# Per-expert gates of an inference step: scattered by adding DMAs into a zeroed DRAM table in place of one-hot products on TensorE

## The chip, the cores and the metric

One core of a Trainium2 chip runs the whole step in one launch. Times are device microseconds, from three runs for the kernel before; a profiled execution is a further run with the hardware profiler on. Lower is better. The engines are PE (TensorE: matmuls, with PEld its weight loads), DVE (VectorE), ACT (ScalarE), POOL (GpSimd) and SP (which only issues DMAs). All DMAs run on the same 16 DMA engines: those that SP issues stand in the profile as hardware_dynamic (q1), those that POOL issues as software_dynamic (q0).

## The reference

The model is one layer: two mixers (RWKV-7 and Mamba-2) and then a product-key expert layer, for 576 tokens (512 of a prompt and 64 of a sample) of width 1024. The change touches only the expert layer:

```python
q = (xn @ w_q).reshape(bsz, t, P_HEADS, 2, P_QDIM // 2)            # 8 heads, 2 sides
s = jnp.einsum('bthcd,ckd->bthck', q, sub_keys).astype(jnp.float32)  # 128 keys a side
sv, si = lax.top_k(s, P_TOPK)                                        # 16 of each side
cand = (sv[..., 0, :, None] + sv[..., 1, None, :]).reshape(bsz, t, P_HEADS, P_TOPK * P_TOPK)
cand_id = (si[..., 0, :, None] * N_KEYS + si[..., 1, None, :]).reshape(bsz, t, P_HEADS, P_TOPK * P_TOPK)
top_s, top_pos = lax.top_k(cand, P_TOPK)                             # 16 of 256 pairs
eid = jnp.take_along_axis(cand_id, top_pos, axis=-1)                 # of 16384 experts
gate = jax.nn.softmax(top_s, axis=-1).astype(xn.dtype)
# for each token and each of its 8 * 16 picks e:
hid = jnp.einsum('td,ted->te', xb, u_tab[eb])
out = jnp.einsum('te,ted->td', jax.nn.gelu(hid, approximate=False) * gb, v_tab[eb])
```

So each token picks 128 of 16384 experts, with a gate for each. An expert that two heads pick for a token gets the sum of both gates.

## The kernel before, in words

**Dense and sparse tokens.** The first 128 tokens (SP) are treated sparsely in the second layer: their 128 picks are gathered row by row. The other 448 tokens (DN) are treated densely: TensorE multiplies them with all 16384 experts, and gates that are zero for all but the picks weigh the hidden values in between. The 16384 experts are 128 "keys" of 128 experts. Each product of 32-bit values is three matmuls on halves (high by high, low by high, high by low: lines 126 to 128, `three_products`); the halves are made by ACT (high) and by POOL or DVE (low).

**The stages, in order of time.** (1) Input projection and the mixers, tile of 128 tokens by tile. Meanwhile SP copies the v table from its argument to scratch in DRAM (`VRows`, 512 KB for each key; `MIX_COPIES` says how many of the 128 copies are issued in which tile: 74 in the mixers, 54 later). (2) Output projection. (3) Routing, `route`: 54 jobs on PE, 16 of them query projections and 38 (`AHEAD4`) hidden keys of the first expert layer that are computed ahead. For each of the eight heads DVE takes the top 16 of each side, then of the 256 sums; POOL's `match_keys` (line 1953) turns ranks into key numbers, two for each head. POOL also makes the low half of every job's weights (`split_low`, line 260), and DVE in `finish_picks` the gates. ACT makes the high half of job j+1 when job j-1 has left PE, and POOL's low half must be there when PE comes to job j+1. (4) Spreading the gates, `spread_gates`: the picks are transposed by PE (`turn_picks`), then for each of the 448 dense tokens DVE compares its 128 picks' first and second keys with a row of key numbers, which gives two 128 by 128 one-hot matrices, one of them scaled by the gates (the scaling is ACT's and DVE's), and PE multiplies them (line 2279): the product is the token's 128 by 128 table of gates. ACT moves it out of PSUM, SP stores it. In between PE computes 14 (`AHEAD5`) further hidden keys. (5) The hidden stage, `act_hidden` and its like: the remaining 76 (`NC_KEYS`) hidden keys; DVE multiplies each key's hidden values with its gates (`make`), and SP stores the product (`prod`). (6) The output stage, `pe_out` and its like: for each key SP loads v (512 KB) and the product w (224 KB), ACT and DVE split both, PE multiplies (24 matmuls). Meanwhile POOL gathers, for the sparse tokens, one value (`value_of_pick`) and one row of v (`row_ring`, 512 KB for 128 tokens) for each of their 128 picks, and DVE adds the weighed row up (line 2711). (7) The last normalization and the stores.

**What sets the order.** Every engine runs its program in order and waits on semaphores; there is no planner. On POOL the order is: splits and matches of the routing jobs, then the splits of hidden keys, then 16 values, then rows and values in turn. A row's gather waits until its slot of 16 (`RING`) is free and until the row three before it has landed (`IN_FLIGHT`). SP's order is written out in `sp_route`, `sp_spread`, `sp_hidden`, `sp_out`.

## Time and profile before

| | |
|---|---|
| median of 3 runs | 2288.07 us (2275.89 to 2293.09) |
| the profiled execution's own time | 2283.04 us |
| its span (first to last instruction) | 2281.2 us |
| granted TensorE clock, mean | 0.977 |
| PE busy | 2184.2 us, 96% |
| DVE busy | 1293.3 us, 57% |
| ACT busy | 882.9 us, 39% |
| POOL busy | 924.2 us, 41% |
| DMA | 478.86 MB, mean 210 GB/s |
| expert layer's stages, from the trace | routing jobs 542 to 922, gates 922 to 1112, hidden 1112 to 1599, output 1599 to 2265 |

A busy share is a mean over stages with different limits: DVE is over 90% busy from 1000 to 1100 us and 15% from 1200 to 1300 us. Matmuls overlap each other in PE, so a matmul's own duration (295 ns) is more than what it adds to the time; how many start in a stretch tells its rate.

### The profile page before, as it was taken

The page shows a single profiled execution, that of the slowest core. Times are in us where ns is not written, and L with a number is a line of the kernel's source. Part 1 is how long each engine was busy: PE and PEld are TensorE (multiplying, and loading weights), DVE is VectorE, ACT ScalarE, POOL GpSimd, SP SyncE. Part 2 cuts the span into 40 slices and gives each one's busy share as a digit, 9 for nine tenths or more (in the row PEclk, how much of TensorE's full clock was granted, in tenths as well). Part 3 has the DMA queues.
Part 4 walks back from the last instruction along what each step waited for, and adds up shares of the span by engine and source line. Part 5 has one row for each costly group of instructions (what it writes and reads, how often), then busy time and mean ns, then how long its engine had stood idle before and what let it go on. Part 6 is the DMA issues. An engine that isn't in the chain of part 4 may idle for free.

```text
span 2281.2 us, 41950 instructions
## 1 busy us (share of the span) xinstructions
PE 2184.2 (96%) x16703; PEld 2069.1 (91%) x16703; DVE 1293.3 (57%) x2471; ACT 882.9 (39%) x1722; POOL 924.2 (41%) x555
## 2 busy tenths in 40 slices
PE   8997888998999999999999999999979999999997
PEld 7996777888999999999999999999759999999996
DVE  4563666656798996899421111112336666666666
ACT  5235445535333333899522222222213333333332
POOL 1433344432445455211233333333765656564300
PEclk9999999898999999999999999999979999999999
DMA  3548366525666566476867677766678888888842
GB/s 129 179 135 242 92 203 190 160 84 171 183 189 193 187 189 187 154 227 218 288 238 256 234 243 239 259 227 224 227 241 275 270 276 275 271 276 269 268 150 82
DMA packets 298806, 478.86 MB, mean 210 GB/s; under 512 B 31168, under 2 KB 227584, under 8 KB 298504
## 3 DMA queue, kind: packets, MB, share of 16 engines
q1 hardware_dynamic: 276104, 409.25, 54.6%
q0 software_dynamic: 22528, 67.19, 9.5%
q8 instruction: 122, 2.00, 0.4%
q14 instruction: 52, 0.43, 0.1%
HBM read 383.86 MB, written 159.60 MB: 238 GB/s over the span
## 4 chain that ended last, share of the span: by engine, by line
PE 73%; DVE 2%; issue 1%; DMA 1%; ACT 1%; POOL 0%; SPq 0%; DVEq 0%; ACTq 0%; POOLq 0%
PE banks L126 22%; PE banks L128 22%; PE banks L127 22%; PE banks L2279 4%; PE banks L1968 1%; DMA u_raw<-arg_u 1%; DVE n_y L342 0%; DMA scratch_gates<-gate_stage 0%; DVE res_x L2763 0%; DVE res_lo L349 0%; DVE n_sq L383 0%; DVE n_inv L335 0%; DVE gates_in L2760 0%; ACT res_hi L1823 0%; POOL u_low L1784 0%
## 5 line engine op out<-in xcount | busy, mean ns | idle before, releaser
L126 PE MATMUL banks<-res_hi,u_high 128*128 128x288 f32 x1456 | 438.2, 301 | 2.8 <-POOL u_low L2156 1.7
L128 PE MATMUL banks<-res_hi,u_low 128*128 128x288 f32 x1456 | 428.9, 295 | 0.0
L127 PE MATMUL banks<-res_lo,u_high 128*128 128x288 f32 x1456 | 428.8, 295 | 0.0
L127 PE MATMUL banks<-w_low,v_high 128*128 128x448 f32 x1024 | 379.3, 370 | 7.7 <-issue 7.7
L126 PE MATMUL banks<-w_high,v_high 128*128 128x448 f32 x1024 | 379.4, 370 | 6.6 <-issue 6.3
L128 PE MATMUL banks<-w_high,v_low 128*128 128x448 f32 x1024 | 379.9, 371 | 5.5 <-issue 5.4
L2156 POOL TENSOR_TENSOR u_low<-u_raw,u_high 128x1024 fp32r<-128x1024 f32 x75 | 181.2, 2416 | 303.8 <-ACT u_high L2152 303.8
L2678 DVE TENSOR_TENSOR gated<-gelu_out,gates_in 128x448 f32<-128x448 f32 x76 | 48.2, 634 | 408.3 <-ACT gelu_out L2635 390.6
L126 PEld LDWEIGHTS banks<-res_hi,u_high 128*128 128x128 f32 x1456 | 273.5, 188 | 3.2 <-POOL u_low L2156 2.0
L127 PEld LDWEIGHTS banks<-res_lo,u_high 128*128 128x128 f32 x1456 | 273.6, 188 | 0.1
L128 PEld LDWEIGHTS banks<-res_hi,u_low 128*128 128x128 f32 x1456 | 273.0, 188 | 0.0
L2788 POOL DMA_INDIRECT row_ring<-scratch_v_rows,expert_of_pick x128 | 188.3, 1471 | 187.4 <-DVE row_total L2711 166.9
L126 PE MATMUL banks<-res_hi,q_wh 128*128 128x288 f32 x864 | 257.7, 298 | 1.4 <-DVE res_lo L349 1.2
L128 PE MATMUL banks<-res_hi,q_wl 128*128 128x288 f32 x864 | 255.3, 295 | 0.0
L127 PE MATMUL banks<-res_lo,q_wh 128*128 128x288 f32 x864 | 255.1, 295 | 0.0
L2626 ACT ACTIVATE w_high<-w_raw 128x448 fp32r<-128x448 f32 x128 | 74.0, 578 | 458.7 <-PE banks L128 400.0
L2671 DVE TENSOR_TENSOR w_low<-w_raw,w_high 128x448 fp32r<-128x448 f32 x128 | 79.9, 625 | 266.3 <-ACT w_high L2626 243.1
L128 PEld LDWEIGHTS banks<-w_high,v_low 128*128 128x128 f32 x1024 | 193.8, 189 | 30.2 <-issue 11.3
L127 PEld LDWEIGHTS banks<-w_low,v_high 128*128 128x128 f32 x1024 | 193.9, 189 | 28.6 <-issue 9.6
L126 PEld LDWEIGHTS banks<-w_high,v_high 128*128 128x128 f32 x1024 | 193.8, 189 | 27.5 <-issue 8.6
L260 POOL TENSOR_TENSOR q_wl<-q_raw,q_wh 128x1024 fp32r<-128x1024 f32 x54 | 130.0, 2409 | 179.3 <-ACT q_wh L256 179.3
L2635 ACT ACTIVATE gelu_out<-banks 128x288 f32<-128x288 f32 x152 | 54.1, 408 | 354.5 <-PE banks L128 354.5
(424 smaller groups left out, 4594.7 us busy)
## 6 DMA issues: line engine op xcount, KB each, us to landing
scratch_v_rows<-arg_v SPq DMA_DIRECT2D x128, 512.0 KB, 8.2
v_raw<-scratch_v_rows SPq DMA_DIRECT2D x128, 512.0 KB
u_raw<-arg_u SPq DMA_DIRECT2D x37, 1024.0 KB, 5.5
scratch_gates<-gate_stage SPq DMA_DIRECT2D x14, 2048.0 KB, 7.5
scratch_prod<-gated SPq DMA_DIRECT2D x128, 224.0 KB, 3.2
w_raw<-scratch_prod SPq DMA_DIRECT2D x128, 224.0 KB
q_raw<-arg_u SPq DMA_DIRECT2D x38, 512.0 KB, 4.0
gates_in<-scratch_gates SPq DMA_DIRECT2D x19, 896.0 KB, 5.0
```

The costliest lines, as they stand in the source:

```text
L126: pe.matmul(out, ah, bh, start=first, stop=False)
L127: pe.matmul(out, ah, bl, start=False, stop=False)
L128: return pe.matmul(out, al, bh, start=False, stop=last)
L260: eng.tensor_tensor(self.wl[:, c % self.ring, :], self.raw[:, c % 3, :], self.wh[:, c % self.ring, :].bitcast(F32), ALU.subtract).then_inc ...
L1968: ins = pe.matmul(bank[0:T, (n % 4) * P:(n % 4 + 1) * P], qT[:, c % 2, tok:tok + T], keys[:, c % 2, :], start=True, stop=True)
L2156: pool.tensor_tensor(self.lo[:, jj % 2], self.raw[:, jj // 2, jj % 2], self.hi[:, jj % 2].bitcast(F32), ALU.subtract).then_inc(self.low, 1)
L2279: ins = pe.matmul(core.psum[:, g % BANKS, t * P:(t + 1) * P], pair[:, g % SLOTS, t, :], pair[:, g % SLOTS, FOUR + t, :], start=True, stop= ...
L2626: act.activation(wh[:, k % W_SLOTS, :], w_raw[:, k % W_SLOTS, :], ACT.Copy).then_inc(w_high, 1)
L2635: ins = act.activation(gelu[:, n % G_SLOTS, half * HALF:(half + 1) * HALF], core.psum[:, 2 * (n % 2) + half, 0:HALF], ACT.Gelu)
L2671: dve.tensor_tensor(wl[:, k % W_SLOTS, :], w_raw[:, k % W_SLOTS, :], wh[:, k % W_SLOTS, :].bitcast(F32), ALU.subtract).then_inc(w_low, 1)
L2678: dve.tensor_tensor(blocks(made[:, m % M_SLOTS, :]), blocks(src), gate, ALU.mult).then_inc(made_done, 1)
L2788: pool.indirect_dma_start(out=ring[:, s % RING, :], out_offset=None, in_=core.v_rows.dst.rearrange("k p d -> (k p) d"), in_offset=bass.Ind ...
```

## The change

The gates' table is made in DRAM by DMAs, without TensorE.

- **Table.** `GateRows`: 128 keys by 128 experts by 448 tokens, 29.4 MB. In the mixers SP writes zeros over it, in 32 DMAs of four keys (eight in each of four tiles) from a row of zeros in SBUF. For that only 40 of the v table's copies remain in the mixers; the 34 others follow the routing's, one with each key of the hidden stage.
- **Places.** For each head, DVE in `finish_picks` computes for every pick its place in the table: (second-side and first-side key numbers as an expert number) times 448, plus the token's number. Three small operations more for each head.
- **Scatter.** `Sparse.scatter`: POOL issues an indirect DMA with `compute_op=ALU.add` for one pick of 128 tokens: 128 elements of 4 bytes. There are 16 for each head for each of three full tiles of tokens. The last tile has 64 tokens: half of its picks are moved to the other 64 partitions (`move`, by SP), so that 8 DMAs do for a head. That makes 448. For one tile, a head's DMAs wait until those of the head before have landed, as two heads may pick one expert.
- **Removed.** `spread_gates` altogether: one-hot matrices, their products, the transposes, the stores of the gates, and also the store of the weighed hidden values with their class `Products`. `AHEAD5` is 0: 90 hidden keys (`NC_KEYS`) follow the routing's last job at once.
- **Hidden stage.** The low half of u is made by DVE in place of POOL from the third key on. SP stores the plain hidden values (`hid_dense`). At key 86, SP waits for all scatters (`scattered`) before the first loads of the output stage.
- **Output stage.** For each key SP loads v, the hidden values and the gates (512, 224 and 224 KB), and DVE multiplies the latter two (`weigh_key`) before they are split. A row's gather no longer waits for the row three before it; it waits until PE is within 8 keys (`AHEAD_ROWS`) of the key at which the row is summed up. `W_SLOTS` is 4 in place of 3.

```diff
-AHEAD5 = 2 * G_STEPS
+AHEAD5 = 0
 AHEAD4 = 38
-MIX_COPIES = (0, 18, 38, 58, N_KEYS - (2 * P_HEADS + AHEAD4))
+KEY4 = N_KEYS - AHEAD4
+MIX_COPIES = (0, 10, 20, 30, 40)
+ZEROED = 4
...
+    def scatter(self, pool, h, n, k):
+        last = n == NT - 1
+        if k == 0:
+            pool.wait_ge(self.placed, h + 1)
+            if last:
+                pool.wait_ge(self.moved, 32 * (h // (P_HEADS // 2) + 1))
+            if h:
+                pool.wait_ge(self.done[n - 1], 16 * h * (TOPK // 2 if last else TOPK))
+        c = h * TOPK + k
+        pool.indirect_dma_start(
+            out=self.core.gate_rows.dst.rearrange("k p t -> (k p t)").unsqueeze(1),
+            out_offset=bass.IndirectOffsetOnAxis(ap=self.place[:, n, c:c + 1], axis=0),
+            in_=self.gates[:, n, c:c + 1], in_offset=None, compute_op=ALU.add).then_inc(self.done[n - 1], 16)
...
+                def copy_and_zero(n):
+                    core.v_rows.copy(sp, MIX_COPIES[n], MIX_COPIES[n + 1])
+                    for z in range(8 * n, 8 * n + 8):
+                        core.gate_rows.zero(sp, zeros, z)
...
+        placed_by = {h: job_of_q[2 * h + 4] + 5 for h in range(P_HEADS - 2)}
+        for j in range(len(jobs)):
+            for _ in range(2):
+                if j < len(jobs) - 1 and placed_by.get(sparse.order[core_n][0], len(jobs)) < j:
+                    core_n += 1
+            scattered_by.append(core_n)
...
                 gemm.split_low(pool, j)
                 if j in match_after:
                     match_keys(*match_after[j])
-            spread.first_low(pool)
+                for h, n, k in sparse.order[scattered_by[j - 1]:scattered_by[j]]:
+                    sparse.scatter(pool, h, n, k)
+            for n in range(2):
+                u.split_low(pool, 0, n)
+            for h, n, k in sparse.order[scattered_by[LAST]:]:
+                sparse.scatter(pool, h, n, k)
...
+                e, f = cleft[:, :, 0:TOPK], cleft[:, :, TOPK:2 * TOPK]
+                link(dve.scalar_tensor_tensor(out=e, in0=picks[:, :, 1, hs], scalar=float(N_KEYS), in1=picks[:, :, 0, hs],
+                                              op0=ALU.mult, op1=ALU.add))
+                link(dve.scalar_tensor_tensor(out=f, in0=e, scalar=float(DN), in1=column[:, :, :].broadcast_to([P, NT, TOPK]),
+                                              op0=ALU.mult, op1=ALU.add))
+                dve.tensor_copy(sparse.place[:, :, hs], f).then_inc(sparse.placed, 1)
...
-def spread_gates(core, acts, u, sel, iota, gelu, gelu_sent_ahead, sel_out, gemm):
...
+                if n == NC_KEYS - 4:
                     core.v_rows.ready(sp)
+                    sparse.scattered(sp)
...
+            sp.dma_start(hid[:, k % W_SLOTS, :], core.hid_dense[k]).then_inc(h_in[k % W_SLOTS], 16)
+            sp.dma_start(gate[:, k % W_SLOTS, :], core.gate_rows.dst[k]).then_inc(g_in[k % W_SLOTS], 16)
...
             def row(s):
                 if s >= RING:
                     pool.wait_ge(summed_rows, s - RING + 1)
-                if s >= IN_FLIGHT:
-                    landed(s - IN_FLIGHT)
+                if ROW_KEY[s] > AHEAD_ROWS:
+                    pool.wait_ge(out_done, ROW_KEY[s] - AHEAD_ROWS)
...
             def _(pool):
                 pool.sem_clear(mixing_sems)
                 project.pool(pool)
-                route.pool(pool, spread)
-                spread.pool(pool)
-                for n in range(2, NC_KEYS):
-                    u.split_low(pool, n // JJ, n % JJ)
+                route.pool(pool)
                 pool_rows(pool)
```

POOL's order in the routing, where two heads' matches meet the jobs' splits (`q_wl` is the low half of a job's weights). Before:

```order
L1953 TENSOR_TENSOR rank_match<-rank_match,top_index_f 128x1280
L260 TENSOR_TENSOR q_wl<-q_raw,q_wh 128x1024
L1953 TENSOR_TENSOR rank_match<-rank_match,top_index_f 128x1280
L260 TENSOR_TENSOR q_wl<-q_raw,q_wh 128x1024 x5
L1953 TENSOR_TENSOR rank_match<-rank_match,top_index_f 128x1280
```

And now:

```order
L2020 TENSOR_TENSOR rank_match<-rank_match,top_index_f 128x1280
L265 DMA scratch_gate_rows<-gate_of_pick,place_of_pick 7340032x1 x2
L307 TENSOR_TENSOR q_wl<-q_raw,q_wh 128x1024
L2020 TENSOR_TENSOR rank_match<-rank_match,top_index_f 128x1280
L265 DMA scratch_gate_rows<-gate_of_pick,place_of_pick 7340032x1 x2
L307 TENSOR_TENSOR q_wl<-q_raw,q_wh 128x1024
```

Two scatters follow every job's split and match, from job 14 to job 52: 78 in all.

POOL's order behind the routing, from the last split of the routing to the first gathers. Before:

```order
L2156 TENSOR_TENSOR u_low<-u_raw,u_high 128x1024 x75
L2775 DMA value_of_pick<-scratch_hid,hidden_of_pick 128x1 x16
L2788 DMA row_ring<-scratch_v_rows,expert_of_pick 128x1024
L2775 DMA value_of_pick<-scratch_hid,hidden_of_pick 128x1
```

And now:

```order
L2221 TENSOR_TENSOR u_low<-u_raw,u_high 128x1024 x2
L265 DMA scratch_gate_rows<-gate_of_pick,place_of_pick 7340032x1 x370
L2568 DMA value_of_pick<-scratch_hid,hidden_of_pick 128x1 x16
L2578 DMA row_ring<-scratch_v_rows,expert_of_pick 128x1024
L2568 DMA value_of_pick<-scratch_hid,hidden_of_pick 128x1
```

The splits of the hidden keys have left POOL, and 370 scatters in one piece stand in their place.

## Rows read from the trace of the kernel before

**Rows 1.** The page: the chain that ended last, by line, share of the span

```profile
PE banks L126 22%; PE banks L128 22%; PE banks L127 22%; PE banks L2279 4%; PE banks L1968 1%; DMA u_raw<-arg_u 1%; DVE n_y L342 0%; DMA scratch_gates<-gate_stage 0%; DVE res_x L2763 0%; DVE res_lo L349 0%; DVE n_sq L383 0%; DVE n_inv L335 0%; DVE gates_in L2760 0%; ACT res_hi L1823 0%; POOL u_low L1784 0%
```

**Rows 2.** Windows: length, busy us (x instructions) by engine, PEclk, DMA share, GB/s

```profile
925.00:1110.00 185.00, 185.00 (x1538) 185.00 (x1537) 172.90 (x252) 173.44 (x478) 33.39 (x14) 1.00 0.68 218
1100.00:1200.00 100.00, 97.22 (x743) 96.83 (x742) 22.79 (x30) 33.75 (x69) 33.85 (x14) 1.00 0.79 274
1142.00:1590.00 448.00, 448.00 (x3383) 448.00 (x3383) 73.56 (x122) 117.60 (x212) 170.09 (x71) 1.00 0.70 243
```

**Rows 3.** Windows of the output stage

```profile
1600.00:1700.00 100.00, 80.43 (x333) 65.95 (x332) 35.45 (x38) 22.31 (x29) 68.28 (x61) 0.85 0.73 239
1700.00:1800.00 100.00, 100.00 (x486) 90.81 (x485) 63.26 (x64) 31.02 (x41) 60.52 (x47) 1.00 0.84 274
2165.00:2240.00 75.00, 75.00 (x365) 68.11 (x364) 43.78 (x45) 22.93 (x30) 0.00 (x0) 1.00 0.44 151
```

**Rows 4.** POOL's gathers of one value: count, busy us, mean ns, idle before

```profile
L2775 POOL DMA_INDIRECT value_of_pick<-scratch_hid,hidden_of_pick x128 | 138.8, 1084 | 50.8 <-issue 50.2 <-DMA row_ring<-scratch_v_rows,expert_of_pick 0.6
```

**Rows 5.** Timeline of POOL's gathers: start, us, engine, line [idle before]

```profile
1620.45 1.94 POOL L2775 DMA_INDIRECT value_of_pick<-scratch_hid,hidden_of_pick  x1 [0.30 <-issue]
...
1677.04 0.94 POOL L2775 DMA_INDIRECT value_of_pick<-scratch_hid,hidden_of_pick  x1 [0.30 <-issue]
1684.78 1.68 POOL L2788 DMA_INDIRECT row_ring<-scratch_v_rows,expert_of_pick  x1 [6.80 <-DVE row_total L2711]
```

**Rows 6.** Timeline of POOL in the routing, one head and the next

```profile
721.56 2.40 POOL L260 TENSOR_TENSOR q_wl<-q_raw,q_wh 128x1024 fp32r<-128x1024 f32 x1 [3.96 <-ACT q_wh L256]
726.08 4.14 POOL L1953 TENSOR_TENSOR rank_match<-rank_match,top_index_f 128x1280 f32<-128x1280 f32 x1 [2.13 <-DVE rank_match L2117]
730.19 2.40 POOL L260 TENSOR_TENSOR q_wl<-q_raw,q_wh 128x1024 fp32r<-128x1024 f32 x1
732.55 2.95 POOL L1953 TENSOR_TENSOR rank_match<-rank_match,top_index_f 128x1280 f32<-128x1280 f32 x1
735.74 2.40 POOL L260 TENSOR_TENSOR q_wl<-q_raw,q_wh 128x1024 fp32r<-128x1024 f32 x1 [0.24 <-ACT q_wh L256]
...
767.15 4.16 POOL L1953 TENSOR_TENSOR rank_match<-rank_match,top_index_f 128x1280 f32<-128x1280 f32 x1 [2.13 <-DVE rank_match L2117]
```

**Rows 7.** Timeline of ACT: it takes the job before PE's current one

```profile
734.00 0.41 ACT L2040 ACTIVATE gelu_ahead<-banks 128x288 f32<-128x288 f32 x1 [4.86 <-PE banks L128]
```

**Rows 8.** Window of that head in the routing

```profile
726.00:767.00 41.00, 41.00 (x310) 40.42 (x309) 37.25 (x136) 14.31 (x25) 21.43 (x8) 1.00 0.60 189
```

**Rows 9.** Landing of transfers at `scratch_hid` (stores, value gathers); DVE's groups by form

```profile
DMA to landing us min/median/max: 1.5/2.5/13.4
...
L2080 DVE TENSOR_TENSOR picks<-pick_values,gate_sum 128x80 f32<-128x80 f32 x8 | 1.9, 242 | 0.3
L2666 DVE TENSOR_TENSOR v_low<-v_raw,v_high 128x1024 fp32r<-128x1024 f32 x91 | 110.8, 1217 | 0.0
L2671 DVE TENSOR_TENSOR w_low<-w_raw,w_high 128x448 fp32r<-128x448 f32 x92 | 57.5, 625 | 164.5 <-ACT w_high L2626 164.1 <-issue 0.4
```

**Rows 10.** DMA queues: packets, MB, share; of 1900 to 2000 us

```profile
q1 hardware_dynamic: 5773, 15.12, 44.7%
q0 software_dynamic: 4026, 12.02, 39.1%
```

**Rows 11.** DMA queues of 1640 to 1660 us, and that window

```profile
q0 software_dynamic: 1351, 3.97, 67.2%
q1 hardware_dynamic: 576, 1.51, 19.1%
...
1640.00:1660.00 20.00, 13.16 (x45) 8.31 (x43) 6.09 (x7) 3.05 (x4) 15.73 (x15) 0.90 0.87 274
```

**Rows 12.** Windows where SP's transfers alone fill the DMA engines

```profile
340.00:360.00 20.00, 19.14 (x298) 15.23 (x297) 12.09 (x24) 13.56 (x28) 11.14 (x10) 1.00 1.08 313
1120.00:1140.00 20.00, 19.31 (x148) 19.08 (x146) 2.39 (x4) 5.93 (x12) 6.15 (x3) 1.00 0.94 347
```

570 lines of the change are left out of this document (168 added, 402 removed).

## The prediction

> **What bounds the kernel now.** I read the chain of waits first: three quarters of the span hang on PE, in the three-product matmuls, and 4% on line 2279, the one-hot products [rows 1]. So the question for each part is what it adds to PE's work or to PE's waits. The windows by stage answer that. In the hidden stage PE never pauses: 3383 matmuls in 448 us, 132.4 ns each, and a hidden key of 48 matmuls takes 6.36 us. In the gates' stage PE is as full (185 of 185 us), but its 1538 matmuls take 120 ns each, because more than half of them are one-hot products [rows 2]. The output stage has three faces [rows 3]: from 1700 us on it runs full at 486 matmuls in 100 us (205.8 ns each, 4.94 us a key of 24), also late where no rows are gathered (365 in 75 us, at a DMA share of 0.44 in place of 0.84). But its first 100 us hold only 333 matmuls, at a granted clock of 0.85. That is where POOL issues gathers without a pause, one in 1.25 us (0.94 and 0.30 idle) [rows 5].
>
> **The sum, against the profiled execution's span of 2281.2 us.**
>
> *One-hot products, removed.* A group is four tokens: 8 one-hot matmul records and 6 of the hidden keys (14 keys of 48 over 112 groups). 185 us for 1538 records make 1.684 us for a group of 14 [rows 2]; its hidden part costs 6 x 0.1324 = 0.794. So 0.890 us x 112 = **-99.7 us**. DVE's and ACT's one-hot work (both over 170 of 185 us busy) goes too, but it lay beside PE. The 14 hidden keys move behind the routing at the same price.
>
> *The hand-over to the hidden stage, removed.* Gates' stores and loads fill the DMA engines, and PE is 97.22 us busy of 1100 to 1200 [rows 2]: **-2.8 us**.
>
> *The burst of row gathers, removed.* 333 in place of 486 matmuls: 153 x 0.2058 = 31.5 us. In 1640 to 1660 POOL's queue holds 67% of the DMA engines' time and SP's only 19% [rows 11], where the steady stage gives SP 44.7% [rows 10]. The new wait lets row 0 go at the second finished key and then one in 0.875 key, so no burst of 16 rows can form: **-31.5 us**.
>
> *Scatters in the routing (78).* The trace has no scatter. The nearest instruction is the value gather, also 128 elements of 4 bytes: 0.94 us and 0.30 idle alone [rows 5], 1.084 and 0.30 on average beside DVE [rows 4], 1.94 at worst of those shown, and 1.68 for a row's gather beside DVE [rows 5]. So c, a scatter's whole price, is 1.25 us at the low end and 1.98 (1.68 and 0.30) at the high end. I take 1.3 to 1.4, nearest to the value gathers' mean. POOL is in order: a scatter delays the next job's low half. One head is six jobs, 41.1 us (match to match, 726.08 to 767.15), in which POOL works 21.4 us [rows 6, 8]; 12 scatters at c = 1.25 make that 36.4, at 1.98 45.2. Even where the total fits, the two matches of a head lie on adjacent jobs. With c = 1.25: match to 730.2, two scatters to 732.7, low half to 735.1, but PE wants it at 734.0 (ACT takes the job before it there [rows 7]); match to 738.1, scatters to 740.6, low half to 743.0, wanted at 734.0 + 1.1 + 6.4 = 741.5. PE loses 2.6 us a head, in the six heads with both matches after job 14: 16 us. With c = 1.98 it is 5.5 us a head, 33 us. Nothing at all is the bound below, if POOL catches up. I take **+18**.
>
> *Scatters behind the routing (370).* They cover 370c. At the end come the last tile's four heads, each waiting until the one before has landed: four times about 2.5 us [rows 9] = 10. They must be done before PE ends its 90 hidden keys (90 x 6.36 = 572 us), less some 8 us for the first loads and splits: 564. The break-even is c = (564 - 10)/370 = 1.50 us. At 1.25 they end 91 us early, at 1.38 43 us, at 1.98 they are 179 us late. With c as taken: **0**. The cover is the hidden stage, which DVE leaves idle but for the u splits (73.6 us busy of 448, with work that mostly goes [rows 2]).
>
> *DVE's added work.* Three operations a head like the 242 ns one [rows 9]: 0.7 us in 41 where DVE is 37.25 us busy [rows 8]. The u split, 1.22 us (as v_low) in a key of 6.36. In the output stage one more product of 0.63 us [rows 9] in 4.94, on 63% busy: 76%. **0** for all. SP issues one load more for a key, ACT nothing: 0.
>
> *Zeros and v copies.* A tile of the mixers had up to 20 copies (10.5 MB) and has 10 copies and 8 DMAs of zeros (12.6 MB). At the 313 GB/s that such a burst reaches that is 7 us more of a full queue, while PE ran 19.14 of 20 us beside it [rows 12]. Nothing below, 4 x 7 = 28 above: **+3**. The 34 copies now in the hidden stage bring it to about 211 GB/s (0.82 MB for u and the stores, 0.52 for the copy, in 6.36 us); before it moved 243 [rows 2]: 0.
>
> *Loads of the output stage.* A key needs 512 + 224 + 224 KB: 199 GB/s, and a row in 0.875 key 121: 320 together, where 274 ran before [rows 3]. In time of the DMA engines: SP's 44.7%, of which 224 of 736 KB (13.6%, a little more as its packets are small) come on top: with POOL's 39.1% [rows 10] 97 to 100%. While rows were gathered no 20 us went above 0.87 [rows 11]; with SP alone the share reached 0.94 and 347 GB/s, and 1.08 [rows 12]. So it is on the edge. If 0.87 is the ceiling, a key takes 4.94 x 0.99/0.87 = 5.62 us for some 112 keys: +76. If 1.0 can be had, 0. The windows of SP's queue alone are the nearer ones, since here too SP's loads are the larger part and the row gathers are evenly paced: **+20**.
>
> The Trainium skill, "DMA: Bandwidth & Descriptors", section "Where 436 GB/s comes from", puts HBM's limit for one core at about 358 GB/s; 320 would pass under it, and by that the term is 0 and the sum 20 us lower. The trace agrees so far that SP's queue alone came to 347 GB/s [rows 12].
>
> Sum: 2281.2 - 99.7 - 2.8 - 31.5 + 18 + 3 + 20 = **2188 us** of span. The profiled execution took 1.8 us more than its span, and the median of the runs lies 5.0 us above that execution: **2195 us**.
>
> **Rivals.**
>
> *A: as above,* 2160 to 2225: 0.48.
>
> *B: the scatters become the bound, slower.* Adding makes each element a read, a sum and a write; nothing in the trace prices that, neither on POOL nor in the DMA engines. Place: SP's wait at key 86, behind which hidden stores, gelu and then PE stand. It bites from c = 1.50; each 0.1 us more costs 37 us there. At 1.98: 2195 - 18 + 33 + 179 = 2389 us. Slower than before by over 1% (2311) needs +116, c of about 1.80. For it: it is a guess between two gathers, and only 20% above what I take is harmless. Against: where POOL ran without a pause the gathers held 0.94 us. 0.28, of which 0.19 above 1.80, 0.06 within 1%, 0.03 still faster.
>
> *C: the output stage is bound by DMA:* 2195 - 20 + 76 = 2251 us. For it, SP was starved at a total share of 0.87 [rows 11]; against, POOL's part there was 67%, now 39%. 0.12.
>
> *D: in the routing every scatter stands behind a DVE operation.* DVE is 37 of 41 us busy there [rows 8]; at the 1.94 us seen once, and 0.30, POOL needs 21.4 + 12 x 2.24 = 48.3 in 41.1 us: 7.2 x 6 = 43 us in place of 18, 2220 us. 0.05.
>
> The Trainium skill, "SBUF — State Buffer", section "SBUF: two separate sides", says that DVE operations on two SBUF ports lock GpSimd out of writing descriptors, with about 3100 ns in place of 620 for a DMA so overlapped; by its figure POOL would need 58.6 us a head and the kernel come to about 2282. The trace shows the lock's direction (0.94 against 1.68) but nothing so long.
>
> *E: routing and loads cost nothing:* 2195 - 18 - 20 = 2157 us. 0.07.
>
> **Range and chances.** 2150 to 2320: the bottom takes in E, the top A, C, D and B up to c of about 1.83; it leaves out most of B's 0.19. About 1% (23 us) is what this kernel's runs tell from no change. Faster: A, C, D, E and 0.03 of B, 0.75. Within 1%: 0.06. Slower: 0.19.
>
> **What the changed profile would show.** Line 2279 gone, hidden keys at 132 ns a matmul up to about 1500 us. Scatters near 0.94 to 1.1 us, the last of 370 by about 1450 us, a gap before the value gathers: if they run into the end of the hidden stage instead, with PE idle behind it, B is right. PE waiting on the low half of q twice a head in the routing: the +18. The first 100 us of the output stage as full as the rest: the -31.5. PE or ACT waiting on v or on the product in the middle of that stage, and a DMA share near 1: C. I am wrong at the root if DMA engines take long over an added element, which POOL's issue times would not show but the landing would.

## The result: slower by 5.4%, and the profile after

The changed kernel takes **2413.86 us** (median of 4 runs, 2391.81 to 2416.62) where the kernel before takes 2287.74: a ratio of **1.054** (95% interval 1.046 to 1.061). I had forecast 2195. Rival B named what came, with a chance of 0.19 for a time more than 1% slower.

The page's group of the scatters (columns as in [rows 4]), and its chain by line, to be held against [rows 1]:

```profile
POOL scratch_gate_rows L265 28%; PE banks L121 11%; PE banks L122 11%; PE banks L123 11%; POOL q_wl L307 1%; POOL rank_match L2020 1%; DMA scratch_gate_rows<-gate_of_pick,place_of_pick 1%; DVE candidates_left L2139 0%; DVE n_y L389 0%; PE banks L2040 0%; DVE pick_pos L2120 0%; DVE candidates_left L2109 0%; DVE pick_pos L2110 0%; DVE pick_values L2106 0%; DVE pick_values L2117 0%
...
L265 POOL DMA_INDIRECT scratch_gate_rows<-gate_of_pick,place_of_pick x448 | 764.0, 1705 | 138.8 <-issue 129.4
```

The three-product matmuls held 66% of the chain before and hold 33% now; POOL's scatters, 1.7 us each and 0.30 idle, hold 28%. What waits for them, in PE's list of waits (us in total, times, longest):

```profile
PE banks L121 <- DVE u_low L2221: 216.8, 2, 211.6
PE banks L121 <- POOL q_wl L307: 20.4, 12, 2.3
```

The 211.6 us are one gap, from 1514.5 to 1726.1. `u_low` is named because DVE's last splits stand in its program behind the product of hidden values and gates, and this waits for the first loads of the output stage, which SP issues only when all scatters have landed. The last scatter starts at 1712.57, and DVE's order behind it is:

```profile
1718.94 0.63 DVE L2476 TENSOR_TENSOR gated<-hidden_in,gates_in 128x448 f32<-128x448 f32 x1 [214.23 <-DMA gates_in<-scratch_gate_rows]
...
1724.76 1.22 DVE L2221 TENSOR_TENSOR u_low<-u_raw,u_high 128x1024 fp32r<-128x1024 f32 x1
```

Three windows, in the columns of [rows 2]: the hidden stage, the gap, and the output stage.

```profile
1200.00:1300.00 100.00, 100.00 (x757) 100.00 (x756) 18.41 (x16) 26.54 (x48) 85.63 (x48) 1.00 0.54 130
1520.00:1712.00 192.00, 0.00 (x0) 0.00 (x0) 0.00 (x0) 0.00 (x0) 153.91 (x100) 0.50 0.21 0
1900.00:2000.00 100.00, 100.00 (x485) 90.82 (x484) 73.38 (x84) 30.69 (x41) 53.96 (x48) 1.00 0.92 322
```

Beside the scatters PE runs full, 132 ns a matmul, as in [rows 2]. Then it does nothing while POOL issues its last hundred. The DMA engines don't hold these up: their share is 0.21. The limit is the time POOL needs to issue one. In the output stage PE runs as full as in [rows 3], at a DMA share of 0.92.

By stages, in us, from the first and last matmuls of each in both traces:

| stretch | before | after | difference | forecast |
|---|---|---|---|---|
| start to first routing job | 542.7 | 544.3 | +1.6 | +3 |
| routing jobs (first to last query matmul) | 379.0 | 409.1 | +30.1 | +18 |
| to the output stage, without the gap | 677.4 | 583.7 | -93.7 | -102.5 |
| gap | | 211.6 | +211.6 | 0 |
| output stage | 666.0 | 645.0 | -21.0 | -11.5 |
| end | 16.1 | 16.2 | +0.1 | 0 |
| span | 2281.2 | 2409.9 | +128.7 | -93 |

The gap is the term that was missed, and the routing cost more than forecast. The -21.0 of the output stage hides two errors that partly cancel (see below). The +1.6 ahead of the routing is within what this stage varies from run to run: the first routing job starts at 537 to 554 us in the traces of this document, with zeros and without. In the routing, the timeline of POOL (start, us) shows the price directly:

```profile
704.58 2.95 POOL L307 TENSOR_TENSOR q_wl<-q_raw,q_wh 128x1024 fp32r<-128x1024 f32 x1
707.70 1.55 POOL L265 DMA_INDIRECT scratch_gate_rows<-gate_of_pick,place_of_pick  x1 [0.17 <-issue]
709.56 1.55 POOL L265 DMA_INDIRECT scratch_gate_rows<-gate_of_pick,place_of_pick  x1 [0.31 <-issue]
710.56 2.97 POOL L307 TENSOR_TENSOR q_wl<-q_raw,q_wh 128x1024 fp32r<-128x1024 f32 x1
```

The kernel before's gather of as many elements held POOL for 0.94 us [rows 5]; a scatter that adds holds it for 1.55. The split behind it is shown with 2.95 us in place of 2.40 [rows 6], but its record begins 0.55 us before the scatter's ends (703.58 + 1.55 = 705.13 for the one at 704.58): behind the scatter it takes its 2.40.

**Two kinds of chips.** The runs below were made on several chips. On some the kernel before takes 2288 to 2292 us, as in the forecast's runs (kind I), on others 2238 to 2241 (kind II). Kernels are compared on one chip only.

### The profile page after: what moved, and what is told of

Same layout as the page of the kernel before. It is cut to its first block, busy times and chain, and to the rows that moved or that the text cites. A ratio compares the mean times of both kernels' runs of the same rounds, so it can differ in the third digit from the quotient of the medians.

```text
span 2409.9 us, 38976 instructions
## 1 busy us (share of the span) xinstructions
PE 2092.1 (87%) x15795; PEld 1980.8 (82%) x15795; DVE 1210.5 (50%) x2320; ACT 726.0 (30%) x1270; POOL 1445.8 (60%) x916
## 3 DMA queue, kind: packets, MB, share of 16 engines
q8 instruction: 125, 2.05, 0.3%
## 4 chain that ended last, share of the span: by engine, by line
PE 34%; POOL 31%; DVE 6%; issue 6%; ACT 1%; DMA 1%; SPq 0%; POOLq 0%; DVEq 0%; ACTq 0%
POOL scratch_gate_rows L265 28%; PE banks L121 11%; PE banks L122 11%; PE banks L123 11%; POOL q_wl L307 1%; POOL rank_match L2020 1%; DMA scratch_gate_rows<-gate_of_pick,place_of_pick 1%; DVE candidates_left L2139 0%; DVE n_y L389 0%; PE banks L2040 0%; DVE pick_pos L2120 0%; DVE candidates_left L2109 0%; DVE pick_pos L2110 0%; DVE pick_values L2106 0%; DVE pick_values L2117 0%
## 5 line engine op out<-in xcount | busy, mean ns | idle before, releaser
L265 POOL DMA_INDIRECT scratch_gate_rows<-gate_of_pick,place_of_pick x448 | 764.0, 1705 | 138.8 <-issue 129.4
L121 PE MATMUL banks<-res_hi,u_high 128*128 128x288 f32 x1456 | 431.1, 296 | 216.8 <-DVE u_low L2221 216.8
L2221 DVE TENSOR_TENSOR u_low<-u_raw,u_high 128x1024 fp32r<-128x1024 f32 x88 | 107.8, 1225 | 452.4 <-ACT u_high L2217 447.3
L2420 ACT ACTIVATE v_high<-v_raw 128x1024 fp32r<-128x1024 f32 x128 | 135.6, 1059 | 639.0 <-PE banks L123 377.7
L2578 POOL DMA_INDIRECT row_ring<-scratch_v_rows,expert_of_pick x128 | 143.1, 1118 | 234.5 <-PE banks L123 183.7
L121 PE MATMUL banks<-res_hi,q_wh 128*128 128x288 f32 x864 | 262.5, 304 | 22.2 <-POOL q_wl L307 20.4
L2465 DVE TENSOR_TENSOR v_low<-v_raw,v_high 128x1024 fp32r<-128x1024 f32 x128 | 156.8, 1225 | 203.3 <-ACT v_high L2420 191.8
L2568 POOL DMA_INDIRECT value_of_pick<-scratch_hid,hidden_of_pick x128 | 154.1, 1204 | 77.5 <-DMA scratch_hid_dense<-gelu_out 38.8
L2434 ACT ACTIVATE gelu_out<-banks 128x288 f32<-128x288 f32 x180 | 64.1, 408 | 438.3 <-PE banks L123 438.3
```

Source lines behind the costliest of these rows:

```text
L121: pe.matmul(out, ah, bh, start=first, stop=False)
L265: pool.indirect_dma_start(out=self.core.gate_rows.dst.rearrange("k p t -> (k p t)").unsqueeze(1), out_offset=bass.IndirectOffsetOnAxis(ap= ...
L2221: pool.tensor_tensor(self.lo[:, jj % 2], self.raw[:, jj // 2, jj % 2], self.hi[:, jj % 2].bitcast(F32), ALU.subtract).then_inc(self.low, 1)
L2420: act.activation(vh[:, k % V_SLOTS, :], v_raw[:, k % V_SLOTS, :], ACT.Copy).then_inc(v_high, 1)
L2434: ins = act.activation(gelu[:, n % G_SLOTS, half * HALF:(half + 1) * HALF], core.psum[:, 2 * (n % 2) + half, 0:HALF], ACT.Gelu)
L2465: dve.tensor_tensor(vl[:, k % V_SLOTS, :], v_raw[:, k % V_SLOTS, :], vh[:, k % V_SLOTS, :].bitcast(F32), ALU.subtract).then_inc(v_low, 1)
```

## The experiments

### What a scatter costs

Theory P: the adding itself costs POOL time. Rival: scatters into DRAM are dear in any form. The first kernel drops the addition:

```diff
-            in_=self.gates[:, n, c:c + 1], in_offset=None, compute_op=ALU.add).then_inc(self.done[n - 1], 16)
+            in_=self.gates[:, n, c:c + 1], in_offset=None).then_inc(self.done[n - 1], 16)
```

> The scatters write their gate without adding it (where two heads pick one expert for a token, one gate is lost). Theory P (the adding itself makes a scatter long to issue: 1.55 us against the 0.94 us of a gather of as many elements): a scatter takes 0.94 us and 0.30 idle, about 1.3 to 1.4 with VectorE's collisions; the last of 370 is issued near 925 + 370 x 1.35 = 1425 us, before the 1500 us at which SP waits for it; TensorE's 212 us gap is gone, the routing loses half of its 30 us, and the kernel takes 2190 us, 5% less than the kernel before. Rival Q (a scatter is long because it writes single elements to DRAM, or because its descriptors queue): it stays at 1.55 us, and the kernel at 2410 us.

Measured on a chip of kind II: 2165.1 us, ratio 0.968 (0.964 to 0.972). Its scatters (count, ns min/median/max, first and last start):

```profile
L265 POOL DMA_INDIRECT scratch_gate_rows<-gate_of_pick,place_of_pick x448: 954/958/2096, 652.4 to 1415.7; - x150
```

0.96 us, near the gather's 0.94. The last goes out some 100 us before the end of the hidden stage (1415.7 against 1523.8) and the gap is gone. **The addition costs POOL 0.60 us for each DMA**; without it the forecast's mechanism holds on this kind of chip. On the other kind it does not, as is shown further down.

Fewer adding scatters, every fourth pick left out:

```diff
+        self.order = [x for x in self.order if x[2] % 4 != 3]
```

> Every fourth pick's scatter is left out (336 in place of 448; a quarter of the gates stays zero), each as long as before. Theory P (POOL's issue time bounds, and only what sticks out behind the hidden stage costs): 258 scatters behind the routing x 2.05 us = 529 us, which ends about 20 to 30 us before SP needs them, so the whole gap of 212 us goes, and the kernel takes about 2195 us. Rival R (half or more of the loss is elsewhere, as in a cold start behind the gap or in DMA traffic): a quarter off the scatters takes a quarter off the loss, and it stays above 2300 us.

Measured (kind II): 2192.3 us, 0.973 (0.968 to 0.979), each still 1.55 where no DVE operation is met, the last at 1502.3, no gap. The break-even was placed rightly; the number of DMAs times their price decides.

Does the price lie in the number of elements? The last tile is not packed, so 128 scatters of 64 elements stand in place of 64 of 128:

```diff
-        self.order += [(h, NT - 1, k) for h in range(P_HEADS // 2, P_HEADS) for k in range(TOPK // 2)]
+        self.order += [(h, NT - 1, k) for h in range(P_HEADS // 2, P_HEADS) for k in range(TOPK)]
...
+        r = slice(0, DEC_SEQ if last else P)
...
-            out_offset=bass.IndirectOffsetOnAxis(ap=self.place[:, n, c:c + 1], axis=0),
-            in_=self.gates[:, n, c:c + 1], in_offset=None, compute_op=ALU.add).then_inc(self.done[n - 1], 16)
+            out_offset=bass.IndirectOffsetOnAxis(ap=self.place[r, n, c:c + 1], axis=0),
+            in_=self.gates[r, n, c:c + 1], in_offset=None, compute_op=ALU.add).then_inc(self.done[n - 1], 16)
```

> The changed kernel with the last tile's scatters not packed: 16 of 64 elements for a head in place of 8 of 128, so 512 scatters and the same number of elements. Theory E (POOL's 1.55 us is 128 times a cost for each element, some 12 ns): a scatter of 64 takes about 0.8 us and 0.30 idle, so the last one ends within 128 x 1.1 - 64 x 1.85 = +22 us of before, 2414 to 2440. Rival F (a fixed price for each DMA): 64 scatters more at 1.85 to 2.05, +118 to +131 us, about 2540.

Measured (kind II): 2479.8 us, where the changed kernel takes 2389.0 on the same chip (below). The timeline of the small scatters:

```profile
1725.60 1.43 POOL L266 DMA_INDIRECT scratch_gate_rows<-gate_of_pick,place_of_pick  x1 [0.30 <-issue]
1727.33 1.43 POOL L266 DMA_INDIRECT scratch_gate_rows<-gate_of_pick,place_of_pick  x1 [0.30 <-issue]
```

1.43 for 64 elements against 1.55 for 128: nearly all of it is a fixed price for each DMA. E fell. F's kind of price held, though it was some 30 us too high: +91 us where it had +118 to +131.

### Where the other 0.20 us come from

Alone a scatter costs 1.85 us with its idle time; on average behind the routing it was 2.05 (370 starts from 954.2 to 1712.6 us). With all 448 behind the routing, stretches with and without DVE's splits can be compared:

```diff
-                if j < len(jobs) - 1 and placed_by.get(sparse.order[core_n][0], len(jobs)) < j:
-                    core_n += 1
+                pass
```

> All 448 scatters are issued behind the routing, none between its jobs. Theory P (the 78 between the jobs cost the routing its 30 us by delaying the low halves): routing's matmuls take 379 us as before the change, not 409; behind it 448 x 2.05 = 918 us, so the gap grows by 78 x 2.05 = 160 us: 2412 - 30 + 160 = 2540 us. Rival S (the routing is longer because VectorE has three operations more for each head): it stays near 409 us, and the kernel takes 2570 us.

Measured (kind II, one run): 2499.7 us. The routing's jobs take 378 us again, so the +30 there was the scatters' and not DVE's. The scatters of 922 to 1490, and those of 1500 to 1800, where DVE does nothing:

```profile
L265 POOL DMA_INDIRECT scratch_gate_rows<-gate_of_pick,place_of_pick x271: 1546/1548/2372, 922.8 to 1489.8; - x136
...
L265 POOL DMA_INDIRECT scratch_gate_rows<-gate_of_pick,place_of_pick x160: 1546/1547/1565, 1499.1 to 1799.2; - x160
```

With DVE idle none is longer than 1.57 us. PE and ACT are idle there too, so this alone doesn't name DVE; the starts do. In the changed kernel's timeline one in three begins inside the split of u:

```profile
1292.05 1.55 POOL L265 DMA_INDIRECT scratch_gate_rows<-gate_of_pick,place_of_pick  x1 [0.30 <-issue]
...
1293.60 1.23 DVE L2221 TENSOR_TENSOR u_low<-u_raw,u_high 128x1024 fp32r<-128x1024 f32 x1 [5.14 <-ACT u_high L2217]
1293.90 2.36 POOL L265 DMA_INDIRECT scratch_gate_rows<-gate_of_pick,place_of_pick  x1 [0.30 <-issue]
1296.57 1.55 POOL L265 DMA_INDIRECT scratch_gate_rows<-gate_of_pick,place_of_pick  x1 [0.30 <-issue]
```

Would more work on DVE cost more? First one further operation of the same form, for 81 keys:

```diff
+                if 6 <= n < NC_KEYS - PRE:
...
+                    dve.tensor_tensor(vl[:, 3, :], u.raw[:, n % JJ // 2, n % 2], u.hi[:, n % 2].bitcast(F32),
+                                      ALU.subtract).then_inc(again, 1)
```

> The changed kernel with a further DVE subtraction of the same form as that for u_low (two SBUF operands, 128x1024, 1.23 us) for 81 of the hidden keys; its result is not used. Theory L (a scatter that meets such an operation takes about 0.8 us more, for POOL is held for its length): the scatters behind the routing take 81 x 0.8 to 1.2 us longer in all, +65 to +97 us, and the gap before the output stage grows by that; time about 2480 to 2510. Rival (the mean of 2.05 against 1.85 comes from something else, such as the hidden stage's transfers): no change, 2414.

Measured (kind II): 2384.3 us against the changed kernel's 2389.0 on the same chip, no change. Theory L fell. Then two more, in a row behind the split:

```diff
+                if 6 <= n < NC_KEYS - PRE:
...
+                    for k in range(2):
+                        dve.tensor_tensor(vl[:, 2 + k, :].rearrange("p (a b) -> p a b", a=2),
+                                          acts.x[:, 0:2, 0:512], acts.hi[:, 0:2, 0:512].bitcast(F32),
+                                          ALU.subtract).then_inc(again, 1)
```

> The changed kernel with two further DVE subtractions (two SBUF operands, 128x1024, 1.23 us each) right behind that for u_low, in 81 hidden keys; their result is not used. Theory L2: a scatter that starts while such an operation runs waits for its end and takes about 1.42 us from there; one that has begun is not touched. With three operations in a row (3.7 us) only two scatters fit in a key of 6.36 us: 3.18 us each in place of 2.12, one of about 5 us and one of 1.55 in turn. By key 86 some 175 of the 370 are out, the other 195 follow at 1.85: the last at about 1875, the gap of PE about 375 us, time about 2550. Theory M (an operation costs a scatter at most some 0.8 us, however many follow): no more than 0.8 us a key, 65 us: about 2450. Rival (no connection with DVE): 2389.

Measured (kind I, one run): 2409.9 us, the changed kernel's time. The added time that L2 and M expected did not come:

```profile
1279.78 1.23 DVE L2221 TENSOR_TENSOR u_low<-u_raw,u_high 128x1024 fp32r<-128x1024 f32 x1 [2.86 <-issue]
1280.92 2.35 DVE L2497 TENSOR_TENSOR v_low<-res_x,res_hi 128x1024 fp32r<-128x1024 f32 x2
1281.21 2.35 POOL L265 DMA_INDIRECT scratch_gate_rows<-gate_of_pick,place_of_pick  x1 [0.30 <-issue]
1283.87 1.55 POOL L265 DMA_INDIRECT scratch_gate_rows<-gate_of_pick,place_of_pick  x1 [0.30 <-issue]
1285.72 1.55 POOL L265 DMA_INDIRECT scratch_gate_rows<-gate_of_pick,place_of_pick  x1 [0.30 <-issue]
```

3.6 us of DVE lengthen one scatter by 0.8 us and leave the next alone. In each of the three kernels a key holds exactly three scatters: 2.35 + 1.55 + 1.55 and three times 0.30 are the key's 6.36 us. POOL falls into step with PE's keys, and while it does the loss is 0.8 us a key with one, two or three DVE operations.

What holds the one scatter can be read from the starts. Of the changed kernel's 263 scatters from 955 to 1510 us, 84 take longer than 1.8 us. All 84 begin while one of DVE's operations over two SBUF operands (1.23 us) is running, and all end 1.42 to 1.44 us after that operation's end: above, 1293.60 + 1.23 + 1.43 = 1296.26. None of the 179 short ones begins inside such an operation. In the kernels with two and three operations the same holds for 84 and 179 each, and there 84 of the short ones run while an operation begins beside them. So the half of L2 that was the mechanism held: **a scatter that begins inside such a DVE operation waits for that operation's end; one that has begun is not touched, nor does a later operation hold it.** What failed was its sum: the wait ends with the operation that was met.

### Is it the same on other chips?

> The changed kernel, once more, beside the kernel before on one chip. If the difference is in POOL's scatters it is the same everywhere: ratio 1.05 to 1.06, scatters of 1.55 and 0.30 us alone, 2.05 in the mean, the last of them some 1058 us after the first of the 370 begins plus or minus 10, PE idle for about 212 us before it. If chips differ in it (another price of adding), the gap would differ by 3.7 us for each 0.01 us.

Measured (kind II): 2389.0 us against 2238.2, ratio 1.065 (1.061 to 1.070). The gap is 212.1 us, the mean scatter 1.71 us: POOL's price is the same. The ratio is worse, since the kernel before is 50 us faster there and the changed kernel only 25. Why that is, is the second question.

### The burst of gathers and the kernel before

I had priced the hole in the first 100 us of the output stage [rows 3] at 31.5 us and put it down to row gathers that starve SP's loads. In that window PE's only waits are 24 on "issue", 19.4 us in all, and none for a load. The kernel before itself once more, on a chip of kind II:

> The kernel before, once more, profiled on this chip. Theory R (the burst of row gathers starves SP's loads and makes the thin first 100 us of the output stage): window 1600 to 1700 holds some 333 matmuls again, DMA queue of SP under 25% in 1640 to 1660. Rival T (an event of that one execution, such as the granted clock falling to 0.5 by itself): the same gathers, 1.25 us apart, but over 480 matmuls in that window. The hidden end to first output matmul as before, 677 us; output stage 622 to 635 us by T, about 660 by R.

```profile
1600.00:1700.00 100.00, 100.00 (x528) 93.66 (x527) 55.49 (x58) 34.22 (x48) 68.81 (x58) 1.00 0.75 259
...
1640.00:1660.00 20.00, 20.00 (x100) 18.55 (x99) 10.89 (x12) 6.12 (x8) 16.04 (x14) 1.00 0.90 300
```

On a chip of kind II the same gathers, 1.25 us apart, make no hole (2236.8 us; T held there), and this at a DMA share of 0.90 where [rows 11] has 0.87 and PE was thin. So it is not the load on the DMA engines that makes it, and it is no wonder that spreading the rows did nothing on such a chip:

```diff
-                if s >= IN_FLIGHT:
-                    landed(s - IN_FLIGHT)
+                if ROW_KEY[s] > AHEAD_ROWS:
+                    pool.wait_ge(out_done, ROW_KEY[s] - AHEAD_ROWS)
```

> The kernel before, with one part of the change: a row's gather waits until TensorE is within 8 keys of its use, and not for the row three before it. Theory P (the unpaced burst of row gathers starved TensorE in the first 100 us of the output stage): those 100 us hold 480 matmuls in place of 333, and the kernel takes 20 to 31 us less, 2257 to 2267 us (ratio 0.986 to 0.991). Rival T (the changed kernel's output stage is shorter by 21 us for another reason, as its four slots for w in place of three or the long pause ahead of it): the burst's hole stays and the time is 2288 us.

Measured: 2238.5 us, 1.000 (0.998 to 1.002). The same edit with `AHEAD_ROWS` 3, this time on a chip of kind I:

> The kernel before, its row gathers paced to within 3 keys of the key that uses them, in place of the wait for the row three before. So no run of gathers 1.25 us apart but the first 16. Theory R (the run of gathers makes the hole): on a chip where the kernel before takes 2288, 2240 to 2260 and over 480 matmuls in 1600 to 1700; where it takes 2240, no change within 0.3%. Rival (the hole comes from the chip alone, whatever POOL does): no change on either.

Measured: 2249.0 us against 2290.0, **0.985 (0.977 to 0.992)**. The window, where [rows 3] had 333 matmuls:

```profile
1600.00:1700.00 100.00, 96.55 (x455) 87.11 (x454) 50.42 (x53) 29.20 (x39) 52.28 (x46) 0.97 0.71 235
```

The time is where theory R had it, and the window is fuller, though not over the 480 that R wanted: on kind I the run of gathers does make the hole. What is left of it lies in the first 40 us of the stage, where the 16 value gathers still go one behind the other, from 1597.4 to 1617.5 us. The changed kernel has the same rest on kind I: POOL issues 20 gathers 1.25 us apart, 16 of them values, and PE has 60 matmuls in 20 us where 97 are full.

```profile
1760.00:1780.00 20.00, 14.78 (x60) 11.30 (x59) 6.26 (x9) 3.05 (x4) 14.97 (x15) 0.89 0.85 301
```

This accounts for the two kinds in the output stage. It takes 666 us in the trace of the kernel before on kind I and 623 on kind II: the hole is 32 of these 43 us, and the rest is a slower pace throughout, 486 matmuls in 100 us against 495. The changed kernel's takes 645 and 622, with 11 us of hole.

### A version that sums first, and PE starved

If adding is dear and a plain scatter cheap, DVE can do the sums. For each head it compares its picks' places with those of all earlier heads, multiplies by their gates, sums, and adds this to the head's gates; scatters are plain, and the later head's overwrites:

```diff
+                lambda ts=ts, shape=shape, same=same: link(dve.tensor_tensor(
+                    same, bc(self.number[:, ts, hs], 3, shape), bc(self.number[:, ts, 0:w], 2, shape), ALU.is_equal)),
+                lambda ts=ts, shape=shape, same=same: link(dve.tensor_tensor(
+                    same, same, bc(self.own[:, ts, 0:w], 2, shape), ALU.mult)),
+                lambda same=same, total=total: link(dve.tensor_reduce(total, same, AX_X, ALU.add)),
...
+                        self.gates[:, ts, hs], self.own[:, ts, hs], total, ALU.add))]
...
-        placed_by = {h: job_of_q[2 * h + 4] + 5 for h in range(P_HEADS - 2)}
+        placed_by = {h: job_of_q[2 * h + 4] + 5 + 2 * h for h in range(2)}
```

> A whole version with plain scatters. Where two heads pick one expert for a token, DVE first adds the earlier heads' gates to the later head's (compare, multiply, sum, add: about 4 us times the head's number, 112 us in all, head 1 in the routing, 2 and 3 at its end, 4 to 7 between the hidden stage's splits), and the later scatter overwrites. Scatters 0.95 and 0.30 us; the last issued between 1420 and 1470, before the loads at key 86 ask for them; no gap of PE before the output stage. If DVE's sums hold the scatters up (each that starts in one waits for its end) they may end up to 60 us later, still hidden. Time by theory P: that of the version with plain scatters and lost sums, 2165, up to 2185 if the routing gets longer by DVE's head 1 and the copies. Rival: DVE's sums push the splits of u behind PE's need, some 20 keys by 3 us: 2225.

Measured (kind I): 2511.0 us, 1.093 (1.086 to 1.100). Theory P and its rival both fell: the last scatter started at 1539, but PE came to the output stage only at 1852.6. Twice more, on another chip of kind I, with the plain version without sums beside it:

> The version with plain scatters (where two heads pick one expert one gate is lost), once more. Theory C (a scatter every 1.25 us starves PE on some chips, whatever DVE does): on a chip where the kernel before takes about 2288 us, PE drops to a matmul in 2 to 3 us in parts of the scatters' time and this takes 2350 to 2550; where the kernel before takes 2240, it takes 2165. Rival D (DVE's sums do it): 2165 to 2215 on any chip.

> The version with plain scatters and DVE sums, once more. Theory C: about 2510 again where the kernel before takes 2288, and about 2170 to 2190 where it takes 2240. Rival D: about 2510 minus the chip's 50 anywhere, 2460.

Measured: **2667.3 us** without sums (2165.1 on kind II), 2532.8 with them. Theory C held and D fell: DVE's sums are not the cause. The version without them, in PE's waits from 950 to 1400 us, that window, and a timeline:

```profile
PE banks L121 <- issue: 122.6, 53, 3.1
...
950.00:1400.00 450.00, 66.21 (x166) 46.29 (x165) 3.68 (x3) 4.96 (x9) 342.50 (x339) 0.50 0.05 11
```

```profile
1111.76 0.28 PEld L123 LDWEIGHTS banks<-res_hi,u_low 128*128 128x128 f32 x1 [2.52 <-issue]
1112.72 0.96 POOL L265 DMA_INDIRECT scratch_gate_rows<-gate_of_pick,place_of_pick  x1 [0.30 <-issue]
1113.16 0.40 PE L123 MATMUL banks<-res_hi,u_low 128*128 128x288 f32 x1 [2.40 <-issue]
1113.98 0.95 POOL L265 DMA_INDIRECT scratch_gate_rows<-gate_of_pick,place_of_pick  x1 [0.30 <-issue]
1114.56 0.28 PEld L121 LDWEIGHTS banks<-res_hi,u_high 128*128 128x128 f32 x1 [2.52 <-issue]
```

While POOL issues, PE does one matmul in 2.8 us in place of one in 0.13: 166 in 450 us. It waits for nothing that the profile shows, the DMA engines' share is 0.05, the granted clock is at 0.50. The same version on kind II, with the same scatters:

```profile
1000.00:1100.00 100.00, 100.00 (x757) 100.00 (x756) 19.60 (x16) 26.09 (x47) 76.18 (x79) 1.00 0.67 212
```

The hole of the kernel before looks like the same thing in small: gathers 1.25 us apart, and PE waiting on "issue" alone. The changed kernel shows nothing of it in the hidden stage, where its scatters are 1.85 us or more apart. Is it the rate? A POOL memset ahead of each plain scatter, short (one column) or longer (256 columns and a wait for its end):

```diff
+                pool.memset(sparse.pause[:, i:i + 1], 0.0)
                 sparse.scatter(pool, h, n, k)
```

> The version with plain scatters, with a POOL memset of one column (about 0.1 us) ahead of each scatter behind the routing, so one in 1.35 to 1.4 us. (Where two heads pick one expert one gate is lost.) If the rate decides with its threshold above 1.4 us: PE is starved while they go, some 480 to 510 us, and the whole takes 2670 to 2700 on a chip where the kernel before takes 2290. If a short free stretch of POOL is enough: below 2250. On a chip where it takes 2240: 2165.

```diff
+                link(pool.memset(sparse.pause[:, 0:256], 0.0))
                 sparse.scatter(pool, h, n, k)
```

> The same with a POOL memset of 256 columns (0.31 us) and a wait for its end, so one scatter in 1.6 to 1.7 us. (Where two heads pick one expert one gate is lost.) The 370 scatters then take 590 to 630 us, some 40 to 75 us more than the hidden stage hides. With the threshold of the rate below 1.6 us: PE at full rate beside them, and 2210 to 2290. With the threshold between 1.7 and 1.85: starved, 2750 or more on a chip where the kernel before takes 2290.

Measured on one chip of kind I, one run each: 2624.3 and **2223.7 us**. Their windows, the short pause first (each scatter with its memset counts two instructions of POOL):

```profile
960.00:1400.00 440.00, 129.32 (x304) 85.36 (x305) 7.35 (x6) 10.92 (x20) 332.09 (x622) 0.50 0.07 19
```

```profile
960.00:1400.00 440.00, 440.00 (x3324) 440.00 (x3323) 84.53 (x69) 115.50 (x210) 360.04 (x547) 1.00 0.51 166
```

311 scatters: 304 matmuls. 273 scatters: 3324, which is full rate. The slower one pays a gap of 53.5 us, since its scatters end late.

The mean of the first, one in 1.42 us, misleads. The short memset fits into the 0.30 us that are idle behind a scatter anyhow, so most follow each other as without it:

```profile
1100.09 0.96 POOL L266 DMA_INDIRECT scratch_gate_rows<-gate_of_pick,place_of_pick  x1 [0.19 <-issue]
1101.04 0.12 POOL L2032 MEMSET pause<- 128x1 f32 x1
1101.35 0.96 POOL L266 DMA_INDIRECT scratch_gate_rows<-gate_of_pick,place_of_pick  x1 [0.19 <-issue]
```

184 of its 309 distances are under 1.3 us. In the second the median is 1.57 and none is shorter. So on kind I **scatters evenly 1.57 us apart do no harm, and ones mostly 1.26 to 1.43 apart starve PE**; where between the two it turns, and whether the distance counts or the wait for the memset's end, these two runs don't tell. The mean alone does not decide: in the hidden stage of the version with sums scatters come one in 1.61 us on average, in long runs 1.26 apart with stops between them, and PE does 1694 matmuls in 540 us:

```profile
960.00:1500.00 540.00, 279.49 (x1694) 257.06 (x1695) 116.84 (x68) 57.74 (x106) 357.21 (x336) 0.70 0.27 85
```

A whole version must avoid long runs and still be done in time. Groups of 9 for two keys, and then 2 or 3 for each half key, with the gathers of the output stage within 3 keys:

```diff
             for i, (h, n, k) in enumerate(sparse.order[scattered_by[LAST]:]):
+                if i % 9 == 0 and i:
+                    pool.wait_ge(sparse.key_done, 2 * (i // 9) - 1)
                 sparse.scatter(pool, h, n, k)
```

> The version with plain scatters and DVE sums, where POOL issues the scatters behind the routing in groups of 9, one group for two hidden keys (11.25 us of 12.72, and what DVE's operations add), so that it pauses for some 1 us now and then; the last group goes at about 1480. Theory C with rate: PE starves only where POOL issues without pause; the starved stretches get shorter or vanish, 2190 to 2300 on a chip like the last, 2170 to 2190 on the others. If a pause of 1 us in 12.7 is not enough: as f_sums.

```diff
+                if i * 4 // 9 > due:
+                    due = i * 4 // 9
+                    pool.wait_ge(sparse.half_done, (due + 1) // 2) if due % 2 else pool.wait_ge(sparse.key_done, due // 2)
                 sparse.scatter(pool, h, n, k)
...
-AHEAD_ROWS = 8
+AHEAD_ROWS = 3
```

> The version with plain scatters and DVE sums, the scatters behind the routing paced by half keys (2 or 3 for each 3.18 us, 4.5 for a key), and the row gathers of the output stage within 3 keys of their use. Theory C with rate: against the version paced by groups of 9 the stretches in which PE is starved get fewer again (they cost it some 60 us in the hidden stage and 20 in the output stage): 2190 to 2260 on a chip where the kernel before takes 2290, 2170 to 2190 where it takes 2240. If an average of 1.41 us a scatter is too fast in itself: 2285 as with groups of 9.

Measured: groups of 9, 2285.6 us against 2290.0, 0.999 (0.995 to 1.003). Half keys, **2235.3 us against 2292.1: 0.978 (0.971 to 0.984)**, with the reference's sums. That is faster than the kernel before on the same chip; the changed kernel did not run there, and took 2413.9 where the kernel before takes 2287.7. Its hidden stage:

```profile
960.00:1500.00 540.00, 517.42 (x3763) 508.16 (x3762) 169.27 (x110) 130.32 (x236) 373.81 (x346) 0.98 0.46 148
```

3763 matmuls where full rate gives 540 / 0.1323 = 4080: it still loses some 42 us. It has one scatter in 1.57 us on average. The pacing did not always make groups of two or three: where POOL is behind, it catches up without a pause. From 1130.8 to 1147.3 us it issues fourteen 1.26 us apart, and these two windows follow each other:

```profile
1120.00:1140.00 20.00, 19.58 (x145) 19.31 (x145) 14.45 (x7) 4.98 (x9) 16.65 (x12) 1.00 0.56 173
1140.00:1160.00 20.00, 12.74 (x62) 11.76 (x61) 2.39 (x3) 1.66 (x3) 12.31 (x13) 0.66 0.43 132
```

Counted over this stage by a scatter's place in such a run (distances under 1.35 us), PE does 7.1 to 7.5 matmuls a us beside the first five, 5.7 beside the eighth and 2.5 beside the ninth; full rate is 7.56. With groups of 9 the eighth has 6.4 and the ninth 3.8. So on these chips of kind I **it takes a run without a pause, and PE is starved from about the eighth scatter of it on.**

How much of the 0.978 is the gates' table and how much the calmer gathers is not separated: the gathers alone gave the kernel before 0.985 on another chip of kind I, and the two intervals overlap. No run of this version on kind II was made.

## Why the forecast was wrong, step by step

- **"Scatters behind the routing (370) ... With c as taken: 0"** is the step that failed. c was taken as 1.3 to 1.4 us, near the value gathers' mean. It is 2.05 over the 370: 1.25 as a gather, 0.60 for the addition (the plain version), and on average 0.20 for the scatter in three that waits for DVE's split. The break-even of 1.50 and the formula were right: 370 x (2.05 - 1.50) = 204 us, and the gap is 211.6. The forecast said itself that nothing in the trace prices the adding; the fault was to take the value of the nearest row as likeliest for an instruction that does more, with a margin of 0.1 to 0.2 us below a cliff of 37 us for each 0.1. Rival B should have led. Its high end, 1.98, came within 25 us.
- **"Scatters in the routing: +18"**: +30, within its bounds 0 to 33. PE waits for `q_wl` 12 times, as many as forecast, 20.4 us in all; where the other 10 us lie was not looked into. With plain scatters the jobs took 393 us (+14), 12.3 us of it PE's waits for `q_wl`; with none in the routing they took 378.
- **DVE's added work at 0**: the cost was under-counted (the multiply-add for the place takes 1.7 us on average, where I had 0.24, and 2.4 to 3.5 us in the four heads in which it meets POOL's split), but the routing's 378 us without scatters show that it lay beside other work.
- **One-hot products and hand-over, -102.5**: -93.7, with PE's restart behind the gap in it. In the version with plain scatters and no gap: 589 us from the routing's last query matmul to the output stage, -88 against 677, with the 11.4 us that PE waits for the first splits of u in it. The size was right within some 14 us.
- **Burst of row gathers, -31.5**: the output stage gained 21. The hole was worth the 31.5 (32 us), but 11 us of it stayed: I thought of the rows alone, and the run of 16 value gathers ahead of them still makes one. With 0 for the loads these are the measured -21; that -11.5 was forecast and -21.0 came is two errors of opposite sign. In the kernel before the pacing alone gave 41 us (0.985); of the 30.7 us between the two profiled executions, on different chips, 25 lie in the output stage. The mechanism I named, SP's loads starved in the DMA engines, was wrong: on kind II the share is as high and there is no hole, and in the plain version PE starves at a share of 0.05. On kind II there was nothing to gain, which is most of why the ratio there is 1.065 and not 1.054.
- **Loads of the output stage, +20**: 0. A share of 0.92 and 322 GB/s go with PE at full rate. The page "DMA: Bandwidth & Descriptors" of the Trainium skill (section "Where 436 GB/s comes from"), with HBM's limit of about 358, gave that 0, and the trace agrees. Rival C fell.
- **Rival D** fell: of the 78 scatters in the routing only 2 take longer than 1.8 us, and their mean is 1.60. The lock was of the right kind but met elsewhere, in the hidden stage, where one scatter in three takes 2.35 us in place of 1.55. The "about 3100 ns" of the Trainium skill, "SBUF — State Buffer", section "SBUF: two separate sides", which the forecast had weighed, appear nowhere; the longest scatter of the changed kernel was 2.85 us.

What the forecast had no thought of: that making the scatters cheaper would, on kind I, starve PE. In this kernel the dear addition keeps the scatters 1.85 us apart, where nothing of it is seen.

**Open:** what starves PE. The profile shows neither a semaphore nor a DMA, and nothing in these runs tells a shortage of instructions from a limit on PE itself. Nor is it known what makes a chip one of kind I. The kinds are sorted by one time alone, and one of the three chips of kind I has the output stage's faster pace of 495 matmuls in 100 us.

## What to carry to other kernels

An instruction that does more than its nearest relative in the trace (an addition in a DMA) is to be measured by itself before a plan rests on it, above all where a small excess meets a cliff: hundreds in one piece, and a whole stage waiting for the last. Indirect DMAs cost the issuing engine a price for each, nearly independent of their size, so their number is what to plan with. And a stream of them is best paced evenly: on chips of kind I one in 1.57 us went unnoticed, runs of up to five 1.26 us apart cost little, and long runs of these hundreds of us.
